# A gated convolution stage projected with tokens in the partitions, its two products turned back on TensorE

## What is computed

```python
C_WIDTH = D_INNER          # 4096
GRID_W, CONV_W = 64, 3

def _conv3(z, w, rows):
    zg = z.reshape(b, rows, GRID_W, ch)
    zp = jnp.pad(zg, ((0, 0), (0, 0), (1, 1), (0, 0)))
    y = zp[:, :, :-2] * w[0] + zp[:, :, 1:-1] * w[1] + zp[:, :, 2:] * w[2]
    return y.reshape(b, L, ch)

def _odd_layer(h, w_in, conv_w, w_out, rows):
    bg, cg, xt, g = jnp.split(h @ w_in, 4, axis=-1)
    y = bg * _conv3(cg * xt, conv_w, rows) * jax.nn.silu(g)
    return y @ w_out
```

## Time and profile before

| | us |
|---|---|
| median of 3 runs | 2830.23 |
| lowest, highest | 2829.93, 2831.89 |
| the profiled execution | 2829.45 |
| its span | 2827.8 |
| TensorE busy | 2710.5 |
| VectorE busy | 1763.5 |
| ScalarE busy | 1281.1 |
| GpSimd busy | 18.4 |

### The profile page before, as it was taken

One profiled execution on the slowest core, in us unless ns is written; L12 is line 12 of the kernel. 1 busy time (PEld: TensorE's weight loads), 2 busy tenths in 40 slices (PEclk: granted clock), 3 DMA queues, 4 the chain that ended last, 5 costly groups with the idle time before them and its releaser, 6 DMA issues.

```text
span 2827.8 us, 49779 instructions
## 1 busy us (share of the span) xinstructions
PE 2710.5 (96%) x19249; PEld 2550.7 (90%) x19249; DVE 1763.5 (62%) x2244; ACT 1281.1 (45%) x1670; POOL 18.4 (1%) x33
## 2 busy tenths in 40 slices
PE   7999999998889799999999999999999999999997
PEld 7998789998878799999999987889999999999886
DVE  6877878886775755555656435566775455555644
ACT  5556444554544444434353333444444444444443
POOL 1000000000000000000000000000000000000000
PEclk9999999999999899999999999999999999999999
DMA  6565766764656455655558545547785555556564
GB/s 188 149 196 163 264 185 199 220 202 140 197 201 206 153 177 172 190 179 163 174 190 266 189 133 170 188 144 258 245 276 180 185 180 183 182 175 191 176 193 138
DMA packets 450700, 534.50 MB, mean 189 GB/s; under 512 B 32955, under 2 KB 343750, under 8 KB 449670
## 3 DMA queue, kind: packets, MB, share of 16 engines
q1 hardware_dynamic: 447840, 522.29, 58.4%
q0 software_dynamic: 2064, 10.11, 1.1%
q10 hardware_dynamic: 662, 0.25, 0.0%
HBM read 530.46 MB, written 2.10 MB: 188 GB/s over the span
## 4 chain that ended last, share of the span: by engine, by line
PE 82%; DVE 7%; ACT 3%; DVEq 3%; DMA 2%; issue 2%; ACTq 0%; SPq 0%
PE banks L1743 17%; PE banks L1745 16%; PE banks L1744 16%; PE banks L1754 8%; PE banks L1755 8%; PE banks L1756 8%; DVE w_lo L1159 2%; ACT w_hi L656 1%; PE banks L2129 1%; PE banks L2146 1%; DVEq L1150 1%; PE banks L1900 1%; DMA w_raw<-in_l_w_out 1%; DMA w_raw<-in_l_w_in 1%; ACT scr_a L777 1%
## 5 line engine op out<-in xcount | busy, mean ns | idle before, releaser
L1159 DVE TENSOR_TENSOR w_lo<-w_raw,w_hi 128x1024 fp32r<-128x1024 f32 (+2 forms) x848 | 974.2, 1160 | 813.1 <-ACT w_hi L656 793.4
L656 ACT ACTIVATE w_hi<-w_raw 128x1024 fp32r<-128x1024 f32 (+2 forms) x848 | 844.5, 1005 | 1092.7 <-PE banks L1745 594.6
L1743 PE MATMUL banks<-act_hl,w_hi 128*128 128x256 f32 x4304 | 1243.3, 289 | 33.7 <-DVE w_lo L1159 14.8
L1745 PE MATMUL banks<-act_hl,w_lo 128*128 128x256 f32 x4304 | 1221.3, 284 | 0.0
L1744 PE MATMUL banks<-act_hl,w_hi 128*128 128x256 f32 x4304 | 1221.0, 284 | 0.0
L1743 PEld LDWEIGHTS banks<-act_hl,w_hi 128*128 128x128 f32 x4304 | 827.6, 192 | 48.4 <-DVE w_lo L1159 16.3
L1744 PEld LDWEIGHTS banks<-act_hl,w_hi 128*128 128x128 f32 x4304 | 827.8, 192 | 3.8 <-issue 2.4
L1745 PEld LDWEIGHTS banks<-act_hl,w_lo 128*128 128x128 f32 x4304 | 827.6, 192 | 0.0
L1754 PE MATMUL banks<-w_hi,act_hl 128*128 128x512 f32 (+3 forms) x1440 | 509.6, 354 | 24.9 <-DVE act_hl L1262 7.4
L1755 PE MATMUL banks<-w_lo,act_hl 128*128 128x512 f32 (+3 forms) x1440 | 506.9, 352 | 0.0
L1756 PE MATMUL banks<-w_hi,act_hl 128*128 128x512 f32 (+3 forms) x1440 | 506.5, 352 | 0.0
(11 more groups left out here) (272 smaller groups left out, 1562.2 us busy)
## 6 DMA issues: line engine op xcount, KB each, us to landing
w_raw<-in_od_w_in SPq DMA_DIRECT2D x256, 512.0 KB, 4.1
w_raw<-in_ev_w_in SPq DMA_DIRECT2D x256, 256.0 KB, 3.6
w_raw<-in_l_w_in SPq DMA_DIRECT2D x96, 512.0 KB, 4.2
w_raw<-in_l_w_in SPq DMA_DIRECT2D x128, 256.0 KB, 3.2
ada_ring<-in_ada_w SPq DMA_DIRECT2D x128, 256.0 KB, 4.3
w_raw<-in_l_w_out SPq DMA_DIRECT2D x64, 512.0 KB, 4.8
y_mix<-in_ada_w SPq DMA_DIRECT2D x128, 256.0 KB, 3.1
const_b<-in_ada_w SPq DMA_DIRECT2D x128, 256.0 KB, 4.8
```

The costliest lines, as they stand in the source:

```text
L656: last = nc.scalar.activation(dst(w_hi[:, p % RING, :]), src(w_raw[:, p % RING, :]), ACT.Copy)
L1159: last = tt(dst(w_lo[:, p % RING, :]), src(w_raw[:, p % RING, :]), dst(w_hi[:, p % RING, :]).bitcast(F32), ALU.subtract)
L1743: mm(out, hi, a[:, kt, 0:T], start=start, stop=False, skip_group_check=True)
L1745: return mm(out, lo, a[:, kt, 0:T], start=False, stop=stop, skip_group_check=True)
```

## The change

Only the stage `conv` and the placing of its last steps are changed. The projection puts tokens in the partitions: for each of the two halves of 128 tokens, one group takes the parts cg and xt (512 columns side by side in the slot) and one takes bg and g (two runs of 256 columns, the first and the fourth of the slot). That is 4 x 3 = 12 matmuls of 512 columns a piece. The banks now hold: 0 and 1 cg and xt of either half of the tokens, 2 and 3 bg and g.

ScalarE copies banks 0 and 1, and of banks 2 and 3 it copies bg and takes the silu of g, half a bank each. VectorE forms cg * xt and bg * silu(g) at piece 3. At piece 2 of the next unit, TensorE turns both products back with eight 128 x 128 transposes into banks 4 and 5. At piece 6 ScalarE copies bank 4 into the padded buffer, and at piece 7 VectorE does the taps and multiplies with bank 5. There are three new semaphores for these steps. In `out3` the last step is moved from piece 7 to 10 (ScalarE) and 11 (VectorE).

```diff
@@ ScalarE, conv @@
                 if p == 2:
                     sc.wait_ge(s["y"], i + 1)
-                    full(sc, "conv", i, 1)
-                    copy(conv_b, bank(A)).then_inc(s_free, 1)
-                    full(sc, "conv", i, 2)
-                    copy(conv_x, bank(B)).then_inc(s_free, 1)
-                    full(sc, "conv", i, 3)
-                    copy(conv_c, bank(C)).then_inc(s_free, 1)
-                    full(sc, "conv", i, 4)
-                    nc.scalar.activation(conv_g, bank(3), ACT.Silu).then_inc(s_free, 1)
+                    for t in range(TT):
+                        full(sc, "conv", i, 1 + t)
+                        copy(conv_cx[:, t, :, :], halves(bank(t))).then_inc(s_free, 1)
+                    for t in range(TT):
+                        full(sc, "conv", i, 3 + t)
+                        copy(halves(conv_b)[:, t, :], bank(2 + t)[:, 0:T])
+                        nc.scalar.activation(halves(conv_g)[:, t, :], bank(2 + t)[:, T:2 * T], ACT.Silu)\
+                            .then_inc(s_free, 1)
+                if p == 6:
+                    sc.wait_ge(s["turned"], i + 1)
+                    copy(conv_z[:, :, :, 1:65], bank(4).rearrange("p (b r n) -> p b r n", b=2, r=4))\
+                        .then_inc(s["padded"], 1)
@@ VectorE, conv @@
                 if p == 3:
                     ve.wait_ge(s_free, all_left("conv", i))
-                    tt(z[:, :, :, 1:65], conv_c.rearrange(rows, b=2, r=4), conv_x.rearrange(rows, b=2, r=4),
-                       ALU.mult)
-                    drain()
+                    tt(halves(conv_p), conv_cx[:, :, 0, :], conv_cx[:, :, 1, :], ALU.mult)
+                    tt(conv_b, conv_b, conv_g, ALU.mult).then_inc(s["prod"], 1)
+                if p == 7:
+                    ve.wait_ge(s["padded"], i + 1)
                     for tap in (1, 0, 2):
...
                         drain()
-                    tt(conv_y, conv_y, conv_b, ALU.mult)
-                    drain()
-                    tt(yt[:, ds(2 * i, 2), :], halves(conv_y), halves(conv_g), ALU.mult).then_inc(s["y"], 1)
+                    tt(yt[:, ds(2 * i, 2), :], halves(conv_y), halves(bank(5)), ALU.mult).then_inc(s["y"], 1)
@@ TensorE, project @@
+                pairs = [w[:, slot, 0:1024].rearrange("p (s n) -> p s n", s=4) for w in (w_hi, w_lo)]
                 for b in range(4):
                     if first:
                         enter(stage, i, 1 + b)
-                    for q in range(2):
-                        r = features(half(b, q), slot, 256 * b + q * P, act, p, first and q == 0, last)
+                    hi, lo = (w[:, 1:3, :] if b < 2 else w[:, 0:4:3, :] for w in pairs)
+                    r = tokens_of(halves(bank(b)), hi, lo, act, p, b % 2, first, last)
@@ TensorE, new step @@
+            def conv(p, i):
+                s = S["conv"]
+                if p == 2:
+                    te.wait_ge(s["prod"], i + 1)
+                    te.wait_ge(s["y"], i + 1)
+                    for b, src in ((4, conv_p), (5, conv_b)):
+                        for f in range(2):
+                            for t in range(TT):
+                                r = nc.tensor.transpose(PS[:, b, f * T + t * P:f * T + (t + 1) * P],
+                                                        halves(src)[:, t, f * P:(f + 1) * P], ident[:, :])
+                    r.then_inc(s["turned"], 1)
@@ TensorE, conv and out3 @@
-                stage_loop(te, "conv", run("conv"), none, nothing)
+                stage_loop(te, "conv", run("conv"), conv, nothing)
-                stage_loop(te, "out3", run("out3"), none, placed({11: [lambda: gates_rows(2)]}))
+                stage_loop(te, "out3", run("out3"), none, placed({2: [step(conv, 2, COUNT["conv"] - 1)], 11: [lambda: gates_rows(2)]}))
@@ out3, ScalarE then VectorE @@
-                    7: [y_ready("conv"), *mixes("out3", 11)],
+                    6: [step(conv, 6, n)],
+                    10: [y_ready("conv"), *mixes("out3", 11)],
...
-                    7: mixes("out3", 11),
-                    9: [lambda: gate_diags(2, 80)]}))
+                    7: [step(conv, 7, COUNT["conv"] - 1)],
+                    11: mixes("out3", 11),
+                    9: [drain, lambda: gate_diags(2, 80)]}))
```

More of the change, by code:

```diff
@@ L297, in build @@
             "four": ("gate", "cols", "cols_sb", "rows", "rows_sb", "o", "y"),
-            "conv": ("y",),
+            "conv": ("prod", "turned", "padded", "y"),
         }.items():
@@ L530, in build @@
         four_c, four_f = view(scr_b[:, 1024:2048], 2, 512), view(scr_b[:, 2048:2560], 2, T)
-        conv_x, conv_g, conv_b, conv_y = (scr_b[:, 512 * n:512 * n + 512] for n in range(4))
-        conv_c = scr_b[:, 2576:3088]
+        conv_cx = scr_b[:, 0:1024].rearrange("p (t s n) -> p t s n", t=TT, s=2)
+        conv_b, conv_y = scr_b[:, 1024:1536], scr_b[:, 1536:2048]
+        conv_p, conv_g = scr_b[:, 2576:3088], scr_b[:, 3088:3600]
         conv_z = scr_b[:, 2048:2576].rearrange("p (b r n) -> p b r n", b=2, r=4)
@@ L1479, in conv @@
                     ve.wait_ge(s_free, all_left("conv", i))
-                    rows = "p (b r n) -> p b r n"
-                    z, v = conv_z, conv_y.rearrange(rows, b=2, r=4)
-                    tt(z[:, :, :, 1:65], conv_c.rearrange(rows, b=2, r=4), conv_x.rearrange(rows, b=2, r=4),
-                       ALU.mult)
-                    drain()
+                    tt(halves(conv_p), conv_cx[:, :, 0, :], conv_cx[:, :, 1, :], ALU.mult)
+                    tt(conv_b, conv_b, conv_g, ALU.mult).then_inc(s["prod"], 1)
+                if p == 7:
+                    ve.wait_ge(s["padded"], i + 1)
+                    z, v = conv_z, conv_y.rearrange("p (b r n) -> p b r n", b=2, r=4)
                     for tap in (1, 0, 2):
```

## The result

The change makes the kernel faster, and the forecast of 2802.5 us was within 0.2% of the time:

| kernel | median of its runs, us | lowest to highest | ratio to before, 95% interval |
|---|---|---|---|
| before | 2830.19 | 2829.93 to 2831.89 | 1 |
| after | 2806.59 | 2804.63 to 2807.16 | 0.9911 [0.9899, 0.9924] |
| after, measured again beside other kernels (before: 2831.41 there) | 2804.86 | 2801.73 to 2807.13 | 0.9909 [0.9892, 0.9925] |

A forecast was written before the change was run, and what follows sets the result against it. TensorE, busy 96% of the span, was taken as the bound. Terms -41.0 + 13.9 + 0 + 1.6 - 2.5 + 0.3 = -27.7 us from 2829.45, with 0.78 for the median, gave 2802.5 us; range 2797 to 2821.

The forecast's parts named there:

- The projection: Stage `conv`, 256 pieces: 12 matmuls of 512 columns at 226.7 ns replace 24 of 256 at 120.0 ns, -41.0 us.
- The other bound: Projection matmuls at 233.1 ns, as where the wide form reads `act2`: a saving of only 21 us.
- rival (a): Split 512-column operand of the third and fourth banks pays the fixed part twice, 20.5 us back: 2823 us; chance 0.10.
- (d): Wide matmuls take 240 ns everywhere, so the projection gains nothing while transposes and bank waits remain: 2843.5 us; chance 0.03.
- Rival (c): Projection matmuls have almost no fixed part to save, gain 10 us against 13.3 paid: about 2833 us; chance 0.04.
- The transposes: Eight uncovered f32 transposes per unit on TensorE after piece 2 of the next unit, 0.87 us each set: +13.9 us.
- The wait for the products: TensorE's transposes wait for two VectorE products, out near 4.9 us and wanted at 8.2: cost 0.
- The banks: ScalarE's table load delays emptying the third bank, TensorE waits 0.4 us in four units: +1.6 us, between 0 and 6.
- Beside the stream: Units 1 to 4, beside `ada_w` loads: taps moved behind piece 7 let weight loads go earlier, removing stalls: -2.5 us.
- rival b: Stalls beside the `ada_w` stream stay or grow, 2 us in four units: 2810 us; chance 0.80 jointly with the forecast.
- Unit 0: First unit of the stage, with VectorE's norm steps between its low halves, may lose a little: +0.2 us, an estimate.
- The medians: The median of the runs was taken as 0.78 us above the profiled execution, turning 2801.8 into 2802.5 us.

The follow-up runs named there:

- the added Silu: Kernel after plus one single-element Silu in unit 0, ahead of the loop over units 1 to 8, removing its sixteen table loads: 2802.88 us.
- the swapped stage: Kernel after with each 512-column projection matmul split into two of 256 columns, tokens still in the output partitions and transposes kept: 2843.11 us, ratio 1.0047.
- the single transpose above: Kernel after with one transpose per unit in place of eight, part of the computation left out: 2791.65 us, ratio 0.9866.

## Why 226.7 and why 233.1

The next kernels only move tensors in SBUF, but for what is said. After itself was measured again beside the first three of them. In the kernels before and after, `w_hi` and `w_lo` start at 34944 and 53376 and `act` at 88192, all multiples of 128, and `act2` at 157792, 96 past one. These addresses are from the compiled programs.

The padding ahead of `act2`:

```diff
+        sb("pad", [P, 8])
         pa = ExitStack()
```

> The kernel after once more, beside the other kernels of this call. The same as measured: 2806.6 us (2804.6 to 2807.2), against which the two paddings and the added Silu are read. If the last pieces of out3's units are at the mercy of when a weight transfer lands, its runs spread over 2 to 3 us.

> The kernel after with 32 unused bytes per partition laid ahead of the tensors of the second half, which moves act2 from SBUF address 157792 (32 past a multiple of 64) to 157824 (a multiple of 64); act stands at 88192, a multiple of 64. Theory: the 233.1 ns against 226.7 ns of rows 6 and 5 is the alignment of the stationary side's rows. Then the first eight pieces of each unit of out2 and out3, 64 in all, go from 2.80 to 2.72 us: 5.0 us less, about 2801.6. Rival: it is the place in SBUF (the upper part, beside other tensors), or the tensor's use in the stage: then nothing moves and these pieces stay at 2.80.

> The kernel after with both the added Silu ahead of the loop and the 32 bytes of padding. If the two are independent and the alignment theory holds: 1.8 + 5.0 = 6.8 us less than the kernel after, about 2799.8 us (2798 to 2802). If the alignment is not the cause: 1.8 us less, 2804.8.

Measured: after again 2804.86 us (2801.73 to 2807.13, a spread of 5.4 where I had expected 2 to 3), with the padding 2799.99 (2799.51 to 2800.62), with padding and Silu 2797.36 (2795.34 to 2799.91), 0.6 under my range. `out3`'s pieces from `act2` take 2.72 us in place of 2.80. Here are two starts, 60 matmuls apart, in its unit 1, all of them from `act2`:

```profile
2654.34 0.39 PE L1760 MATMUL banks<-w_hi,act_hl 128*128 128x512 f32 x1
...
2667.94 0.39 PE L1760 MATMUL banks<-w_hi,act_hl 128*128 128x512 f32 x1
```

226.7 ns. By the medians 32 bytes of padding are worth 4.9 us, where 5.0 were forecast; no run with the padding is as long as the shortest of after. So the tensor's place sets the spacing, and not its use.

The other way round, `act` moved off:

```diff
+        sb("pad_a", [P, 8])
         act = sb("act_hl", [P, KT, 2 * T], F32R)
+        sb("pad_b", [P, 8])
```

> The kernel after with 32 unused bytes ahead of act and 32 behind it, so that act stands at 88224 (32 past a multiple of 64) and act2 where it stood by that measure (157856, 32 past). It is the other end of the prediction's bound for the 512-column matmul, made by hand. Alignment theory: the projection stage's pieces go from 2.72 to 2.80 us, 256 x 0.08 = 20.5 us, the other stages that hold act as the stationary side lose 6 to 9 more: 2833 us (2827 to 2840), slower than the kernel before would be predicted. Rival (place or use of act2): nothing moves, 2806.6.

Measured: 2812.25 us (2811.36 to 2813.50). The projection did what the theory said:

```profile
2394.80 0.40 PE L1761 MATMUL banks<-w_hi,act_hl 128*128 128x512 f32 x1
...
2408.80 0.40 PE L1761 MATMUL banks<-w_hi,act_hl 128*128 128x512 f32 x1
```

14.00 us over 60, 233.3 ns, and the stage is 18.2 longer. The sum was still wrong by 21 us, because of something that I had not expected: the stage begins at 1871.80 us and not at 1882.97. In the stages ahead of it `act` is the moving side of 256-column matmuls, and those became faster (116.7 to 117.8 ns in place of 120.0). Two kernels ask which side counts. One has the kernel before with the same two paddings:

> The kernel before with 32 unused bytes ahead of act and 32 behind it, so that act stands 32 past a multiple of 64 while every other tensor keeps its place by that measure. Here act is the moving side of the 256-column matmuls, not the stationary one. In the kernel after with the same padding the stages ahead of the convolution ended 9 to 11 us earlier. Theory: a moving side that is off by 32 bytes runs faster (about 117 ns in place of 120.0 a matmul of 256 columns), so part of what the wide matmul saves lies in the placement of act: projection stage 6144 x 2 to 3.5 ns = 12 to 21 us less, the stages ahead of it 10 less, out3's last eight pieces 2.6 more: 2803 to 2812 us. Rival: the earlier stages gained by something else that the padding moved, and the 120.0 ns stay: 2820 us.

Measured: 2806.15 us (2805.07 to 2809.41), ratio 0.9916 [0.9903, 0.9930]. Its projection, two starts 120 matmuls apart in unit 7 and two in unit 11:

```profile
2209.33 0.28 PE L1745 MATMUL banks<-act_hl,w_hi 128*128 128x256 f32 x1
...
2223.33 0.28 PE L1745 MATMUL banks<-act_hl,w_hi 128*128 128x256 f32 x1
...
2389.99 0.28 PE L1745 MATMUL banks<-act_hl,w_hi 128*128 128x256 f32 x1
...
2404.12 0.28 PE L1745 MATMUL banks<-act_hl,w_hi 128*128 128x256 f32 x1
```

116.7 ns and 117.8 ns in place of 120.0. The stage takes 732.8 us, and the stages ahead of it 12.2 less. So two paddings of 32 bytes, with no other edit, made the old kernel as fast as the change did. The stalls beside the stream grew there from 0.8 us to the 1.8 below, which fits matmuls that reach the low halves sooner:

```profile
PE banks L1745 <- DVE w_lo L1161: 1.8, 6, 0.4
```

The other kernel is after with the weights moved by 32 bytes:

```diff
+        sb("pad_a", [P, 8])
         w_hi = sb("w_hi", [P, RING, SLOT], F32R)
         w_lo = sb("w_lo", [P, RING, SLOT], F32R)
+        sb("pad_b", [P, 8])
```

> The kernel after with 32 unused bytes ahead of w_hi and 32 behind w_lo, so that both weight tensors stand 32 past a multiple of 64 and all others as before. In the projection stage the weights are now the moving side, in the stages of 256-column matmuls the stationary one. If only the stationary side's alignment costs and a moving side off by 32 bytes gains: the projection stage's 226.7 ns fall by 2 to 4 ns (6 to 12 us over 3072) and its piece to 2.68 or less, the stages with stationary weights lose: about 1800 us of them at 2 to 5% would be over 30 us, so 2825 to 2850. If it is the two addresses' difference that counts and not the single address: 226.7 becomes 233.1 and 120.0 becomes 117, near 2812 as with act moved by 32. If the weights' place does not matter: 2805.

Measured: 2809.84 us (2809.19 to 2810.09). The projection:

```profile
2392.92 0.40 PE L1761 MATMUL banks<-w_hi,act_hl 128*128 128x512 f32 x1
...
2406.92 0.40 PE L1761 MATMUL banks<-w_hi,act_hl 128*128 128x512 f32 x1
```

233.3 ns again, the stages ahead fast again (start at 1869.91), and `out3`'s pieces from `act2`, which now is 32 off like the weights, at 2.72. So neither side's own address counts, but the difference of the two. That was the second of the three cases I gave, for which I had 2812.

Then each side placed for its stage: the projection reads its input from `act2`, and the stages ahead go on reading `act`, which is off. This kernel and the next also have the Silu ahead of the loop, and in `out3` the two tensors change places: the first eight pieces of a unit read `act`, the last eight `act2`.

```diff
-                    r = tokens_of(halves(bank(b)), hi, lo, act, p, b % 2, first, last)
+                    r = tokens_of(halves(bank(b)), hi, lo, act2, p, b % 2, first, last)
...
-            norm5 = (5, lambda f: modc[:, 2, f:f + 1], lambda f: ada_x[:, 48 + f:49 + f], act)
+            norm5 = (5, lambda f: modc[:, 2, f:f + 1], lambda f: ada_x[:, 48 + f:49 + f], act2)
```

> The kernel after with the added Silu, with act 32 bytes past a multiple of 64 (it is the moving side in the stages ahead of the convolution) and act2 at a multiple of 64; the projection stage takes its normed input from act2, and out3 its first half from act and its second from act2. From the runs so far: the stages ahead of the projection as in the kernel with act moved (start at 1871.8 us, less 2.6 for out2's aligned half), the rest as in the kernel with both the Silu and the padding, plus 2.6 for out3's half in act: about 2787 us (2784 to 2791). Rival: the projection reads slower from act2's place in any case (2.80 us a piece): 2807.

Measured: 2811.40 us (2809.97 to 2813.63), 24 above what I expected and 4 above the rival that I had named (the projection is slow from `act2` in any case, 2807). The stages ahead were fast (start at 1869.76), but the projection ran at 233.3 ns:

```profile
2391.81 0.40 PE L1765 MATMUL banks<-w_hi,act_hl 128*128 128x512 f32 x1
...
2405.81 0.40 PE L1765 MATMUL banks<-w_hi,act_hl 128*128 128x512 f32 x1
```

The three paddings had put `act2` at 157888. That is a multiple of 64, which was my rule, and not of 128. In the padded kernel above it had been 157824, a multiple of both. So two readings were left: the step is 128, or `act2` is slow for this stage. The last kernel tells them apart. It has one padding, ahead of `act`, which gives 88224 and 157824:

> As the kernel in which the projection stage reads its input from act2 and the stages ahead of it from act, with one padding of 32 bytes in place of three: act stays 32 bytes off (88224), act2 goes from 157888 to 157824. The weight tensors start at multiples of 128 (34944, 53376); 157888 is a multiple of 64 and not of 128, 157824 is one of 128. Theory: what counts is whether the two operands of a matmul start at the same place modulo 128 (or a larger power of two that these addresses also share): same gives 226.7 ns for 512 columns and 120.0 for 256, different gives about 233 and 117. Then the projection's piece is 2.72 us again, out2's and out3's pieces from act2 too, and the stages ahead stay as fast as with act off: start of the projection about 1867 us, then 915 us as in the kernel with Silu and padding, plus 2.6 for out3's half in act: 2786 us (2783 to 2790). Rival: 512-column matmuls from act2 and act behave by something else than the addresses (the buffer's use, its neighbours); then 2.80 us stay and the time is near 2808.

Measured: **2789.36 us** (2785.98 to 2791.30), ratio to before 0.985 [0.9834, 0.9867], the fastest of all, within the range and 3.4 over its middle. The projection is back at 226.7 ns, with the stages ahead still fast (start at 1870.83):

```profile
2379.20 0.39 PE L1763 MATMUL banks<-w_hi,act_hl 128*128 128x512 f32 x1
...
2392.80 0.39 PE L1763 MATMUL banks<-w_hi,act_hl 128*128 128x512 f32 x1
```

Every case in one table (starts past a multiple of 128; spacing in ns where the operand is used, from the pieces' lengths):

| kernel | weights | `act` | `act2` | projection | 512 columns from `act2` |
|---|---|---|---|---|---|
| before | 0 | 0 | 96 | 256: 120.0 | 233 |
| after | 0 | 0 | 96 | 512: 226.7 | 233 |
| `act2` aligned | 0 | 0 | 0 | 512: 226.7 | 227 |
| after, `act` off | 0 | 32 | 32 | 512: 233.3 | 233 |
| before, `act` off | 0 | 32 | 32 | 256: 116.7 to 117.8 | 233 |
| after, weights off | 32 | 64 | 32 | 512: 233.3 | 227 |
| projection from `act2`, three paddings | 0 | 32 | 64 | 512: 233.3 | 233 |
| projection from `act2`, one padding | 0 | 32 | 0 | 512: 226.7 | 227 |

Same start modulo 128: 226.7 and 120.0. Different start: 233.3, and 116.7 to 117.8. No case contradicts this, and the stages ahead agree (`out0` reads `act`: 226.7 before, 233.3 with `act` off). What stays open: the step may be 256 or 512, since the pairs that start alike agree modulo these too. It is not larger, because the two token tiles of `act` lie 512 bytes apart and are equally fast. And nothing here shows why it is so, or why the sign turns with the width.

The table also bounds what the width is worth. Where the operands start alike, two narrow matmuls take 240.0 ns and a wide one 226.7. Where they don't, two narrow ones take 233.3 to 235.6 and a wide one 233.3, so the width saves 2.3 ns at most, and the rewrite still pays its transposes. The two kernels with `act` off show it: the stage takes 732.8 us with the narrow projection and 737.5 with the wide one. Their times, 2806.15 and 2812.25, are ratios of 0.9916 [0.9903, 0.9930] and 0.9931 [0.9915, 0.9948] to before, and the intervals overlap. On that layout the rewrite gains nothing.

## Why the prediction was right, and where not

**The projection** was the term that decided, and the choice in it (226.7 from `act`, not 233.1 from `act2`) was right, for a reason that I only half had. I took the row with the same source tensor. What counts is where that tensor lies against the weights, and the tensor stayed where it was. The other bound was real: with `act` moved by 32 bytes the pieces took 2.80. So there was luck in the term: 32 bytes of another tensor ahead of `act` would have brought the spacing that I had put beside rival (a), at 0.10.

**Rivals (a) and (d)**, split reading and a wide form at 240 ns, are out by the even 226.7. **Rival (c)**, no fixed part to save, is out by the narrow form of the swapped stage (120.0) and the wide one (226.7); it is what happens where the operands start unlike. The Trainium skill (TensorE: Matmul & The Clock Gate, Back-to-back issue gap) gives N/2.4 + 2.5 ns for the gap of a single matmul. These matmuls, each with its own stationary load, take 13.3 ns over N/2.4 at either width when the operands start alike. For them the trace decides against that figure.

**The transposes** were put at 0.87 a unit and cost 0.90: the 0.03 is in the piece behind them, which I had not counted. 0.109 each is confirmed. The prediction has this number from 0.65 / 6; the 0.57 for six starts in its bracket does not give it. The Trainium skill (TensorE: Matmul & The Clock Gate, Part 4: PE-mode transpose) has about 275 ns for one in a kernel. As the length of a record that agrees with the 0.27 us of the single transpose above; what one costs in a row of them is its spacing, 0.109. The granted clock of unit 11, with its eight transposes, is 1.00.

**The wait for the products** is 0, as forecast. The slack is as forecast too: in unit 4, which starts at 2065.71, the second product runs from 2069.76 for 0.69, so it is out at 4.7 us, and the transposes come at 8.3.

**The banks** cost 0.45 and not 0.4 in each of the four units I named. The silu ends at +1.58 and not at +1.7, but the first matmuls behind the wait are slower, which I had not counted. The other four units lose 0.07 each, which I had at nothing. That is no bank wait, since the kernel without the table loads keeps it: the first piece behind the condition sums is 0.14 over a plain one, where before it was 0.07.

**Beside the stream** (rival b) the 2.5 us went, and the moved taps did what was said. VectorE and the sync engine of after in unit 4:

```profile
2069.76 0.69 DVE L1487 TENSOR_TENSOR scr_b<-scr_b 128x512 f32<-128x512 f32 x1
...
2071.86 0.55 SPq L479 DMA_DIRECT2D w_raw<-in_od_w_in  x1
...
2085.18 0.69 DVE L1500 TENSOR_TENSOR y_mix<-scr_b,banks 128x512 f32 x1 [0.17 <-issue]
2085.79 0.75 DVE L1154 SCALAR_TENSOR_TENSOR acc_x<-const_b,silu_c,acc_x 128x512 f32<-128x512 f32 x1
2086.70 1.23 DVE L1165 TENSOR_TENSOR w_lo<-w_raw,w_hi 128x1024 fp32r<-128x1024 f32 x1 [0.16 <-issue]
```

The weight load goes out at +6.15 (forecast +6.3, before +10.05). The low half of piece 8 is ready at 2087.93 and TensorE starts on it at 2088.52: a lead of 0.6 in this unit, 0.6 to 1.3 in the four. I had 1.0. The cover is thin, and it held.

**What was missed** is 2.9 us in the table. The change's part of it is 1.0: 0.5 on the transposes and 0.5 in the first pieces. The rest:
- *Unit 0*, +0.7 where I had 0.2. In it the clock stays low for longer. The first row of the windows above has it: for 5.2 us from the stage's first matmul the granted clock is 0.50, the 1.2 GHz level. TensorE had been idle for 3.50 us and 1.71 us in the norm ahead. Its timeline in after:

```profile
1878.41 1.22 PE L1957 MATMUL banks<-scr_b,ones 128*128 128x128 f32 x4 [3.50 <-DVE scr_b L1199]
...
1882.97 0.79 PE L1759 MATMUL banks<-w_hi,act_hl 128*128 128x512 f32 x1 [1.71 <-DVE act_hl L1227]
1883.56 0.63 PE L1760 MATMUL banks<-w_lo,act_hl 128*128 128x512 f32 x1
...
1887.83 0.63 PE L1761 MATMUL banks<-w_hi,act_hl 128*128 128x512 f32 x1
```

From 1883.56 to 1887.83 ten matmuls start, 0.427 us each. Before, 256 columns took 0.213 there, so the wide form gains nothing at this level. The Trainium skill (TensorE: Matmul & The Clock Gate, Back-to-back issue gap) gives N/1.2 for it; the trace agrees. The level lasted 4.6 us from the stage's first matmul before and 5.6 after. At half the speed the 1.0 more costs 0.5 of the 0.7. In the other profile of after it lasted 6.2, and in that of after with `act` off 3.4, so this part differs from one execution to the next and is not shown to be the change's. The other 0.2 is the saving of one piece, which the row on the spacing counts and this level does not give. VectorE's norm steps, for which I had the 0.2, cost nothing: from the third piece on each takes 2.72.
- *The last piece of `out3`'s unit 0*, +0.7. TensorE waits there for VectorE, which waits in line for ScalarE's high half, which waits for a weight transfer:

```profile
2651.74 1.06 ACT L657 ACTIVATE w_hi<-w_raw 128x1024 fp32r<-128x1024 f32 x1 [2.44 <-DMA w_raw<-in_od_w_out]
...
2653.97 1.28 DVE L1515 TENSOR_TENSOR scr_b<-banks,scr_b 128x512 f32<-128x512 f32 x2
...
2654.71 0.51 PE L1759 MATMUL banks<-w_hi,act_hl 128*128 128x512 f32 x1 [1.83 <-DVE scr_b L1515]
```

Before, the idle 2.44 was 1.54 and the 1.83 was 1.11, and the piece took 3.99 us. With the same code it took 4.71 in the first profile of after and 3.69 in the second, so the 0.7 goes with when a transfer lands and not with the new code.
- *The medians* stand 0.2 and 2.0 us above after's profiled execution. I had 0.8, so the first median lies 2.9 and 1.2, together 4.1 us, over the forecast. The two profiles of after, 2.9 us apart (spans 2802.9 and 2800.0), show where executions of one kernel differ: 2.2 ahead of the stage, which starts at 1882.97 in one and 1880.74 in the other, and 1.0 in the piece above, less 0.3 in unit 0. What makes the 2.2 is open. It is also three times the +0.7 ahead of the stage in the table, so that row says nothing of the change.

## What to carry to other kernels

On a TensorE that is busy all the time, count starts per column, not busy time: one 512-column matmul in place of two of 256 gave 41.0 us here, two and a half times the 16.5 that the transposes and first pieces took back. It gave that only because the operands start alike; with unlike starts the same rewrite gains nothing. Put a first use of an activation function ahead of the loop that uses it, so that no table load stands between full banks and the next unit. And before you rewrite a matmul stage, try the placement of its operands: 64 bytes of padding moved the old kernel as much as the rewrite did, and width, Silu and placement together gave 1.5%.

## What the hardware showed that I had not expected

- The spacing of matmuls depends on how the starts of the two operands in SBUF stand to each other. Alike modulo 128: 226.7 ns for 512 columns and 120.0 for 256. Unlike: 233.3 and 116.7 to 117.8. Over the whole program, `act` off by 32 bytes brought 24.6 us to the kernel with narrow matmuls in the projection (2830.79 to 2806.15) and cost 7.4 us in the one with wide ones (2804.86 to 2812.25).
- With unlike starts the advantage of the wide matmul is gone: 233.3 ns against 233.3 to 235.6 for two narrow ones, where alike it is 226.7 against 240.0.
- At the 1.2 GHz level the fixed part is not there: 427 and 213 ns, 512 and 256 columns at 1.2 GHz exactly, so a wide matmul gains only at the upper level. The placement does not count there either: the kernels with unlike starts show the same 427 and 213 in their first piece.
- Eight 128x128 transposes of f32 pass between wide matmuls at 0.109 us each and leave the clock alone: it is 1.00 over a unit that holds eight.
